# Third attention of a three-layer block: keys and values projected first, the mask added on TensorE, maxima taken per head from PSUM, scores placed among products

## The reference, cut to what matters

```python
def swa_mixer(x, w_qkv, sinks, w_out, pos):
    q, k, v = jnp.split(x @ w_qkv, SWA_SPLITS, axis=-1)   # 1024, 128, 128 columns
    q = partial_rope(q.reshape(B, S, 16, 64), pos)
    k = partial_rope(k.reshape(B, S, 2, 64), pos)
    v = v.reshape(B, S, 2, 64)
    o = sliding_window_gqa_sinks(q, k, v, sinks)
    return o.reshape(B, S, 1024) @ w_out
...
    s = jnp.einsum('bnqhgd,bnkhd->bnhgqk', qb, kk) * scale
    s = jnp.where(mask, s, -jnp.inf)          # window of 128 positions
    mx = jnp.maximum(jnp.max(s, axis=-1), sink)
    e = jnp.exp(s - mx[..., None])
    w = e / (jnp.sum(e, axis=-1) + jnp.exp(sink - mx))[..., None]
    out = jnp.einsum('bnhgqk,bnkhd->bnqhgd', w, vv)
```

## Time and profile before

| | us |
|---|---|
| median of 3 runs | 2053.14 (2051.26 to 2057.03) |
| profiled execution, whole | 2062.65 |
| its span, first to last instruction | 2060.9 |
| PE busy in the span | 1961.6 (95%) |
| DVE busy | 1395.9 (68%) |
| ACT busy | 1129.9 (55%) |
| mean granted clock of TensorE | 0.954 of full |

### The profile page before, as it was taken

One profiled execution on the slowest core, in us unless ns is written; L12 is line 12 of the kernel. 1 busy time (PEld: TensorE's weight loads), 2 busy tenths in 40 slices (PEclk: granted clock), 3 DMA queues, 4 the chain that ended last, 5 costly groups with the idle time before them and its releaser, 6 DMA issues.

```text
span 2060.9 us, 26596 instructions
## 1 busy us (share of the span) xinstructions
PE 1961.6 (95%) x10038; PEld 1608.1 (78%) x10051; DVE 1395.9 (68%) x1162; ACT 1129.9 (55%) x991; POOL 59.2 (3%) x81
## 2 busy tenths in 40 slices
PE   8978999999999998798999999999999999999987
PEld 6756998786789976686778778778787877888875
DVE  4444776444454545537888878888788888888875
ACT  5333554352243433514666767767676676776762
POOL 2230000100000000000000000000000000000000
PEclk8979999998899999778999999999999999999999
DMA  6604445442245545113999989999999999999980
GB/s 232 203 31 143 160 166 184 154 143 82 82 149 203 193 134 184 62 42 104 359 333 325 360 315 346 349 326 355 333 349 347 321 345 326 345 356 329 351 296 31
DMA packets 251591, 486.93 MB, mean 236 GB/s; under 512 B 14108, under 2 KB 19292, under 8 KB 251536
## 3 DMA queue, kind: packets, MB, share of 16 engines
q1 hardware_dynamic: 244976, 477.30, 65.9%
q0 software_dynamic: 6560, 8.91, 1.5%
HBM read 484.05 MB, written 1.05 MB: 235 GB/s over the span
## 4 chain that ended last, share of the span: by engine, by line
PE 59%; DMA 14%; DVE 13%; ACT 7%; issue 4%; DVEq 2%; SPq 0%; POOL 0%; ACTq 0%; POOLq 0%
DMA w_raw<-in_moe_w_down 8%; DVE w_lo L887 7%; PE psum L1908 7%; PE psum L1910 7%; PE psum L1909 7%; PE psum L1500 6%; PE psum L1502 6%; PE psum L1501 6%; ACT w_hi L521 6%; DMA w_raw<-in_moe_w_gate_up 6%; PE psum L1531 3%; PE psum L1533 3%; PE psum L1534 3%; PE psum L1551 2%; PE psum L1654 1%
## 5 line engine op out<-in xcount | busy, mean ns | idle before, releaser
L887 DVE TENSOR_TENSOR w_lo<-w_raw,w_hi 128x2048 fp32r<-128x2048 f32 (+2 forms) x475 | 1029.7, 2196 | 354.5 <-ACT w_hi L521 351.0
L521 ACT ACTIVATE w_hi<-w_raw 128x2048 fp32r<-128x2048 f32 (+2 forms) x475 | 862.3, 1838 | 273.4 <-DMA w_raw<-in_moe_w_gate_up 105.7
L1908 PE MATMUL psum<-w_hi,xg_hi 128*128 128x512 f32 x896 | 361.0, 403 | 0.8 <-DVE xg_lo L1333 0.4
L1909 PE MATMUL psum<-w_lo,xg_hi 128*128 128x512 f32 x896 | 355.1, 396 | 0.0
L1910 PE MATMUL psum<-w_hi,xg_lo 128*128 128x512 f32 x896 | 355.0, 396 | 0.0
L1531 PE MATMUL psum<-xt_hi,w_hi 128*128 128x256 f32 (+1 forms) x840 | 235.2, 280 | 2.5 <-DVE w_lo L887 1.9
L1533 PE MATMUL psum<-xt_lo,w_hi 128*128 128x256 f32 (+1 forms) x840 | 234.7, 279 | 0.0
L1534 PE MATMUL psum<-xt_hi,w_lo 128*128 128x256 f32 (+1 forms) x840 | 234.5, 279 | 0.0
L1908 PEld LDWEIGHTS psum<-w_hi,xg_hi 128*128 128x128 f32 x896 | 169.0, 189 | 41.4 <-DVE w_lo L887 2.5
L1910 PEld LDWEIGHTS psum<-w_hi,xg_lo 128*128 128x128 f32 x896 | 168.9, 189 | 41.0
L1909 PEld LDWEIGHTS psum<-w_lo,xg_hi 128*128 128x128 f32 x896 | 169.2, 189 | 37.9
(11 more groups left out here) (362 smaller groups left out, 2041.6 us busy)
## 6 DMA issues: line engine op xcount, KB each, us to landing
w_raw<-in_moe_w_gate_up SPq DMA_DIRECT2D x224, 1024.0 KB, 6.7
w_raw<-in_moe_w_down SPq DMA_DIRECT2D x96, 1024.0 KB, 7.0
w_raw<-in_w_up SPq DMA_DIRECT2D x22, 1024.0 KB, 5.6
w_raw<-in_ffn_w_gate_up SPq DMA_DIRECT2D x22, 1024.0 KB, 5.5
w_raw<-in_moe_w_down SPq DMA_DIRECT2D x32, 512.0 KB, 4.5
w_raw<-in_w_in SPq DMA_DIRECT2D x12, 1024.0 KB, 6.7
w_raw<-in_ab_w_in SPq DMA_DIRECT2D x12, 1024.0 KB, 5.2
w_raw<-in_w_down SPq DMA_DIRECT2D x10, 1024.0 KB, 6.3
```

Of the source, the lines that this page charges most:

```text
L521: return act.activation(o, i, func, **kw)
L887: TT(w_lo[:, k % RING, 0:n], w_raw[:, k % RING, 0:n], w_hi[:, k % RING, 0:n].bitcast(F32), ALU.subtract)\
L1908: mm(o, hi[:, q, :], wh, start=(q == first), stop=False)
L1909: mm(o, hi[:, q, :], wl, start=False, stop=False)
```

## The change

1. `SWA_BLOCKS` orders the projection as keys and values, queries 0 to 511, queries 512 to 1023.
2. Keys are rotated, doubled and turned while PE makes the first query block, and the first eight query heads while it makes the second.
3. The mask is kept in 16 bits (`mask_16`), with an identity in 16 bits (`ident_16`). For each head PE first multiplies the two into the bank, 384 columns, and the score multiplications add to that.
4. `swa_max` takes a head's two maxima from PSUM, and one more DVE instruction gives the negative of the larger of maximum and sink. ACT reads the scores from PSUM, too. The ring has three banks, and a bank is free when ACT has read it (`at_p`).
5. The scores of heads 0 to 5 of group 0 stand in the last chunk of products of the second query block. Those of group 1 stand between the turned probabilities and PV of group 0.
6. All four chunks of `c_out` are rounded within the attention, two of them in DVE's program behind the last maxima and behind each group's division.

```diff
+SWA_BLOCKS = [(SWA_K, 2 * N_KV * DH), (0, NB), (NB, NB)]
...
+                pool.tensor_copy(mask_16[:], mask_swa[:])
+                pool.tensor_copy(ident_16[:], ident[:])
...
+            def swa_prob(g, h):
+                act.wait_ge(S("at_negm"), 8 * g + h + 1)
+                b_, smx_ = scr[:, (8 * g + h) % 3, :], smx2[:, g]
+                for t, (c0, c1) in enumerate(((0, P), (P, SCW))):
+                    copy((s_first, s_more)[g][:, h, c0:c1], b_[:, c0:c1], ACT.Exp, bias=smx_[:, 1, t, h:h + 1],
+                         accum_out=smx_[:, 2, t, h:h + 1])
+                act.drain().then_inc(S("at_p"), 1)
...
+                round_to(c_sw + 7)
+                for h in range(5):
+                    swa_prob(0, h)
+                swa_block(q1_b)
+                for h in range(5, 8):
+                    swa_prob(0, h)
+                s1 = 2 * (q1_b[0] % 2)
+                turned_queries(1, psum[:, s1:s1 + 2, :])
+                swa_sink(0)
+                round_to(c_sw + 8)
...
+            def swa_max(g, h):
+                b_, smx_ = scr[:, (8 * g + h) % 3, :], smx2[:, g]
+                dve.wait_ge(S("at_qk"), 8 * g + h + 1)
+                dve.reduce_max(smx_[:, 0, 0, h:h + 1], b_[:, 0:P], AX_X)
+                dve.reduce_max(smx_[:, 0, 1, h:h + 1], b_[:, P:SCW], AX_X)
+                dve.drain()
+                TS(smx_[:, 1, :, h:h + 1], smx_[:, 0, :, h:h + 1], sink[:, 8 * g + h:8 * g + h + 1], -1.0, ALU.max, ALU.mult)
...
+                for h in range(3):
+                    swa_max(0, h)
+                round_to(c_sw + 7)
+                for h in range(3, 6):
+                    swa_max(0, h)
+                wait_evacuated(dve, q1_b[0])
+                rotate(NB, 8)
+                dve.sem_inc(S("rotated"), 1)
+                for h in range(6, 8):
+                    swa_max(0, h)
+                swa_sink(0)
+                turned_prob(0, 0)
+                for h in range(8):
+                    if h < 7:
+                        turned_prob(0, h + 1)
+                    swa_max(1, h)
+                swa_sink(1)
+                attended(0)
+                round_to(c_sw + 8)
+                for h in range(8):
+                    turned_prob(1, h)
+                attended(1)
+                round_to(c_sw + 9)
...
+                def swa_qk(g, h):
+                    n = 8 * g + h
+                    if n >= 3:
+                        pe.wait_ge(S("at_p"), n - 2)
+                    b_ = scr[:, n % 3, :]
+                    q_, k_ = qk2[lane(h), 4 * g + h // 2, :], qk2[lane(h), 8 + g, :]
+                    mm(b_[:, 0:SCW], ident_16[:], mask_16[:], start=True, stop=True)
+                    mm(b_[:, 0:P], q_[:, 0:P], k_[:, 0:P], start=False, stop=True, skip_group_check=True)
+                    mm(b_[:, P:SCW], q_[:, P:SEQ], k_, start=False, stop=True, skip_group_check=True).then_inc(S("at_qk"), 1)
...
+                rows_chunk(q1_b, 1, xh, xl, between=scores_between)
+                swa_qk(0, 6)
+                swa_qk(0, 7)
+                turn_queries(1, 2 * (q1_b[0] % 2))
+                pe.wait_ge(S("qk2_ready"), 3)
+                swa_turn(0, 0)
+                for h in range(8):
+                    if h < 7:
+                        swa_turn(0, h + 1)
+                    swa_qk(1, h)
+                    swa_pv(0, h)
+                for h in range(8):
+                    swa_turn(1, h)
+                    if h:
+                        swa_pv(1, h - 1)
+                swa_pv(1, 7)
```

More of the change, by code:

```diff
@@ L98, in weight_plan @@
         ("ple0", ple(0)),
-        ("qkv", project(w["qkv"], KD, SWA_IN)), ("c_out", project(w["c_out"], KD, D)),
+        ("qkv", [wide(w["qkv"], KD, n0, n) for n0, n in SWA_BLOCKS]), ("c_out", project(w["c_out"], KD, D)),
         ("moe", []), ("ple1", ple(1)),
@@ L661, in _, with swa_sink @@
                 root(3)
[L664 to L672, removed]
+            def swa_prob(g, h):
[5 more added lines that the diff above has]
+                act.drain().then_inc(S("at_p"), 1)
+            def swa_sink(g):
+                act.wait_ge(S("sink_ready"), g + 1)
+                copy(smx2[:, g, 4], smx2[:, g, 3], ACT.Exp)
                 act.drain().then_inc(S("at_sum"), 1)
@@ L792, in _ @@
             if "qkv" in live:
-                operand(7)
[L794 to L804, removed]
@@ L805, in _, with swa_block @@
-                for g in range(2):
-                    softmax(g, (s_first, s_more)[g], smx2[:, g])
+                kv_b, q0_b, q1_b = phase["qkv"]
+                c_sw = chunk0["qkv"]
+                def swa_block(block_):
+                    bb, cc, n0, n, ps = block_
+                    wait_used(act, cc + len(ps))
+                    for t in range(NT):
+                        i = copy(p2[:, t, n0:n0 + n], acc[bb % 2][t][:, 0:n])
+                    i.then_inc(S(f"acc_free{bb % 2}"), 1)
@@ L1502, in rows_chunk @@
                         m = mm(o, lo(k, t), wh, start=False, stop=(k == kmax))
+                    if between:
+                        between(k)
                 m.then_inc(S("w_used"), 1)
@@ L1870, in _ @@
[L1870 to L1875 removed]
+                kv_b, q0_b, q1_b = phase["qkv"]
+                lane = lambda h: slice(DH * (h % 2), DH * (h % 2 + 1))
@@ new lines, in _ @@
+                products(kv_b, 0, xh, xl)
+                wait_acc(q0_b[0])
+                rows_chunk(q0_b, 0, xh, xl)
+                pe.wait_ge(S("rotated"), 1)
+                for f in range(2):
+                    for t in range(NT):
+                        i = turn(scr[:, 3, f * SEQ + t * P:f * SEQ + (t + 1) * P], kdup[:, t, f, :, :].rearrange("p u n -> p (u n)"))
+                i.then_inc(S("swa_t"), 1)
+                rows_chunk(q0_b, 1, xh, xl)
+                wait_acc(q1_b[0])
```

181 lines of the change are left out of this document (91 added, 90 removed).

## The result

The changed kernel is slower. Its median is 2065.68 us over 20 runs (2053.56 to 2077.44), that of the kernel before 2056.81 us over 20 runs (2042.96 to 2072.57). The ratio is 1.0047 with a 95% interval of 1.0025 to 1.0069, about 5 to 14 us more. I had forecast 8.0 us more in the stage and put it on a median of 2053.14 us from three runs: 2061.1 us. The measured median is 4.6 us above that.

A forecast was written before the change was run, and what follows sets the result against it. PE was taken to lose about 12 us waiting for DVE and ACT, and by half clock. The stage summed 28.0 + 1.3 + 6.3 + 9.4 + 31.5 + 3.9 + 13.2 + 0.4 = 94.0 against 86.0: 2061.1 us, range 2047 to 2066.

The forecast's parts named there:

- the part up to head 5: Projection with turns and six heads of scores: 28.0 + 1.3 + 6.3 us, ending at 847.9 us.
- the part behind it: From head 5 to the loop of group 0: waits, two heads and query turns, 9.4 us, ending at 857.3.
- the wait for DVE's split: Behind the loop of group 0, PE waits for DVE's division, chunk split and copy: a new 3.9 us.
- the dear price: A head's two score multiplications cost 0.85 us at full clock, 1.60 at half, since the mask separates heads.
- rival 1: Scores keep their old price, 0.36 us at full clock and 0.83 at half: 2053.1 us, no change; chance 0.20.
- the base of the sum: The stage's 8.0 us more was added to the earlier kernel's median, 2053.1 us, giving 2061.1.
- the term of 3.77 us a head: Loop of group 0 at half clock: turns 0.64, mask 0.36, scores 1.60, PV 1.17; eight heads 30.2 us.
- The six heads among the products: Scores of heads 0 to 5 in the last projection chunk: 1.05 us each, 6.3 us together.
- The four waits: PE waits before head 6 (1.0 us), second rotation (2.1), turned queries' copy (2.5) and DVE's split and copy (3.9).
- the new loop is nearest to the ones that stayed: Loop of group 0: the clock stays at 0.50, as in earlier loops that were busy at half clock.

The follow-up runs named there:

- the pairs: Changed kernel with the scores of an even and an odd head issued together, two masks then four multiplications: stage 82.4 us against 96.0.
- The kernels kept warm: Filler multiplications in PE's waits: changed kernel, its c_out split also made late, 2041.01 us (ratio 0.9944); kernel before, 2036.71 us (0.9930).

## Why the prediction was right and wrong

**The direction and the places were right.** PE entered the loop 45.05 us after the first product (850.84), forecast 45.0. That close a match is luck: the part up to head 5 came out 0.8 us longer and the part behind it 0.8 shorter. The clock was at 0.50 in the loop, the wait for DVE's split was there (3.45, forecast 3.9), and PE waited for neither ACT nor DVE in the loop. The scores took the dear price of the earlier trace rows and not that of the earlier trace rows: 1.57 in the loop and 0.85 in the chunk (forecast 1.60 and 0.85). The run without the mask shows why, and the pairs show it the other way round. The Trainium skill, "TensorEngine Tiling (Array Packing)", section Key Properties, says that different tiles can work in parallel. The four multiplications of two heads in 1.59 us agree. So rival 1 is out.

**Wrong was the size, in two terms: the base of the sum and the price of a head in the loop.** The larger error is the base: 3.7 us of the 4.6 us by which 2065.68 exceeds the forecast. I put the stage's 8.0 us on the median of three runs, 2053.14, and over 20 runs it is 2056.81. Executions of this kernel spread over 30 us, so three of them don't fix a median to 4 us. The profiled execution, 2062.65, stood above it and could have warned me. My step "the stage is the same work in every run, so I add to the median" is fine for the difference and says nothing for the base.

The second is the term of 3.77 us a head. It measured 4.00, so 1.8 us over eight heads, of the 2.0 us by which the whole stage exceeds the forecast. The mask was 0.46 instead of 0.36 and PV 1.33 instead of 1.17, the scores 1.57 instead of 1.60. Mask and PV both hold a step between multiplications on 128 rows and on 64: the mask's time runs up to the first score on 64 rows, and PV, on all 128 rows, stands behind the scores. I took the mask's price from fillers that follow one another, and PV's from a loop in which PV follows turns. In the changed kernel's own second loop, where PV follows turns, it is 1.17 again. The six heads among the products were 1.11 each for the forecast's 1.05. The four waits came out 1.7 us lower together (0.42, 1.71, 2.20 and 3.45 for 1.0, 2.1, 2.5 and 3.9), which hid a part of it.

Other differences between the two executions (the second attention 6.2 us shorter, what follows the stage) are not the forecast's, and the measured 5 to 14 us agree with 10.0 of the stage as with 8.0.

**The reason for half clock was wrong, though the clock was as forecast.** The step was "the new loop is nearest to the ones that stayed". Those rows show loops which began at 0.50 and stayed there. I read them as if such a loop couldn't run at 1.00. It can, for 16 us and more, if the clock is up when it begins, and turns and PV alone hold it too, for 7.5 us in the changed order and for 17.1 us, with a few fillers between, in the order before. In this stage, what goes ahead of a loop decides: with the waits left idle it began at 0.50, with fillers in them at 1.00. A wait isn't needed for a fall: in the second attention PE was busy without a break from 482 to 514 us, and the clock went from 1.00 to 0.50 at about 494, in the scores of the earlier trace rows. The Trainium skill, "TensorE: Matmul & The Clock Gate", section Why this matters for your kernels, asks for a TensorE kept busy. I had weighed it against the old loop, busy 28.6 of 30 us at 0.50, and found it against the trace. The kernels kept warm agree with it. The changed kernel's own loop does not: PE was busy in 32.40 of 32.40 us, and the clock stayed at 0.50. What stays true of the earlier trace rows is the other half: a full but loose loop that starts at 0.50 didn't come up in 30 us, while the loop with pairs did.

**What the change itself won and lost.** It meant to take PE out of about 12 us of waits. By the stages at full clock (73.1 and 70.9) it ends 2 us behind. The order before needs PE for less: no masks, and its scores come in pairs by themselves. Its waits don't go away: they are filled with 63 multiplications of 0.21 us, 13 us that nobody uses. The changed order needs 27 of them. What it saves there it pays again in masks and single scores. The clock behind the waits cost 15 us of the 86, and six groups of fillers buy that back without moving anything.

## What to carry to other kernels

Look at the clock behind a wait, not at the wait alone. A wait of 2 to 5 us of TensorE can cost less than the 10 to 30 us at half clock that follow, and multiplications that nobody reads, put into it, gave 0.7% here where the new order lost 0.5%.

When work is interleaved, keep together what shares the array: 64-row multiplications of both halves side by side. Pulled apart by something on all rows they cost twice as much, and each step between the kinds costs 0.14 to 0.16 us more at half clock here.

A price taken from a row holds for its neighbours in that row: take it where the same kind of work stands ahead.

## What the runs showed of the hardware

- Loops of turns and PV at 1.00 (7.5 us, PE busy 7.45) and the same loops at 0.50 for 30 us (PE busy 28.6): both persisted. What differed was what stood ahead. I had not expected that full clock persists there.
- The same instructions behind the same idle wait went two ways, twice: 1.50 us with 1.00 held and with a fall 2 us later, and 1.18 us in the second attention likewise. In the third attention each wait of 1.6 us and more left unfilled had half clock in it or behind it. That is no limit for the rest of the program. Near its end PE waits 1.65 us for DVE (`xt_lo`) in all 14 traces: the clock fell within 2 us in three of them (the kernel before among them) and held in eleven (the changed kernel among them). A wait of 1.91 us shortly before, in the changed kernel, had full clock for the next 5 us and more. What tips it is open.
- A second head's scores on the other half of the rows are free at both clocks: 1.59 us for two and 1.57 for one at half clock, 0.87 and 0.85 at full.
